# First FFN norm: eight ones-matmuls a quarter become one, with the squares added up on VectorE and GpSimd

## What is computed

```python
def rmsnorm(x, w):
    xf = x.astype(jnp.float32)
    y = xf * lax.rsqrt(jnp.mean(xf * xf, axis=-1, keepdims=True) + EPS)
    return (y * w.astype(jnp.float32)).astype(x.dtype)

def swiglu(h, w_gate, w_up, w_down):
    return (jax.nn.silu(h @ w_gate) * (h @ w_up)) @ w_down

x = x + (0.5 * swiglu(rmsnorm(x, p['norm_ffn1']), ...)).astype(x.dtype)
```

## Time and profile before

| | us |
|---|---|
| median of three runs (2019.36 to 2021.33) | 2020.1 |
| the profiled execution, own time | 2022.36 |
| its span in the profile | 2020.5 |
| TensorE matmuls busy in the span | 1983.1 (98%) |
| VectorE / ScalarE / GpSimd busy | 1184.3 / 780.5 / 229.9 |

### The profile page before, as it was taken

One profiled execution on the slowest core, in us unless ns is written; L12 is line 12 of the kernel. 1 busy time (PEld: TensorE's weight loads), 2 busy tenths in 40 slices (PEclk: granted clock), 3 DMA queues, 4 the chain that ended last, 5 costly groups with the idle time before them and its releaser, 6 DMA issues.

```text
span 2020.5 us, 36315 instructions
## 1 busy us (share of the span) xinstructions
PE 1983.1 (98%) x15393; PEld 1928.7 (95%) x15393; DVE 1184.3 (59%) x1640; ACT 780.5 (39%) x1268; POOL 229.9 (11%) x285
## 2 busy tenths in 40 slices
PE   7999999999999999999999999999999999999999
PEld 7899999999999989868899989999999999999999
DVE  5955655556776752565354283377555565577674
ACT  6433333334433342564333393243333333343331
POOL 0000000000000340250011162100000000000000
PEclk9999999999999999999999999999999999999999
DMA  4222232224976515211011133312322223388664
GB/s 153 81 87 102 87 115 96 87 102 175 372 278 235 211 43 192 83 50 43 25 42 43 58 90 130 133 45 100 116 87 84 100 100 116 117 316 324 251 218 161
DMA packets 67042, 265.05 MB, mean 131 GB/s; under 512 B 7564, under 2 KB 20284, under 8 KB 57536
## 3 DMA queue, kind: packets, MB, share of 16 engines
q1 hardware_dynamic: 51648, 198.89, 27.2%
q0 software_dynamic: 15232, 63.83, 8.2%
HBM read 203.52 MB, written 59.18 MB: 130 GB/s over the span
## 4 chain that ended last, share of the span: by engine, by line
PE 92%; DVE 4%; ACT 3%; issue 1%; DMA 1%; POOL 0%; SPq 0%; DVEq 0%; ACTq 0%
PE ps L169 85%; PE ps L1485 1%; PE ps L1529 1%; PE ps L1511 1%; PE ps L247 1%; DVE sb_x L509 0%; DVE sb_xl L563 0%; PE ps L2123 0%; PE ps L2111 0%; PE ps L2089 0%; DVE sb_xl L499 0%; DMA sb_x<-x 0%; PE ps L2105 0%; PE ps L2116 0%; DVE sb_x L548 0%
## 5 line engine op out<-in xcount | busy, mean ns | idle before, releaser
L169 PE MATMUL ps<-sb_xh,sb_up_hi 128*128 128x272 f32 x2400 | 691.9, 288 | 6.4 <-DVE sb_x L2448 2.0
L169 PE MATMUL ps<-sb_xl,sb_up_hi 128*128 128x272 f32 x2400 | 692.2, 288 | 0.0
L169 PE MATMUL ps<-sb_xh,sb_up_lo 128*128 128x272 f32 x2400 | 690.2, 288 | 0.0
L169 PEld LDWEIGHTS ps<-sb_xh,sb_up_hi 128*128 128x128 f32 x2400 | 453.0, 189 | 7.8 <-DVE sb_up_lo L454 2.3
L169 PEld LDWEIGHTS ps<-sb_xh,sb_up_lo 128*128 128x128 f32 x2400 | 452.5, 189 | 0.0
L169 PEld LDWEIGHTS ps<-sb_xl,sb_up_hi 128*128 128x128 f32 x2400 | 452.2, 188 | 0.1
L169 PE MATMUL ps<-sb_h_hi,sb_down_hi 128*128 128x272 f32 x1188 | 342.6, 288 | 0.4 <-DVE sb_down_lo L1049 0.4
L169 PE MATMUL ps<-sb_h_hi,sb_down_lo 128*128 128x272 f32 x1188 | 342.7, 288 | 0.0
L169 PE MATMUL ps<-sb_h_lo,sb_down_hi 128*128 128x272 f32 x1188 | 341.8, 288 | 0.0
L169 PE MATMUL ps<-sb_nh,sb_whi 128*128 128x362 f32 (+1 forms) x696 | 231.0, 332 | 2.4 <-DVE sb_nl L376 1.5
L169 PE MATMUL ps<-sb_nl,sb_whi 128*128 128x362 f32 (+1 forms) x696 | 228.3, 328 | 0.0
(11 more groups left out here) (334 smaller groups left out, 2692.3 us busy)
## 6 DMA issues: line engine op xcount, KB each, us to landing
sb_down_raw<-wb SPq DMA_DIRECT2D x92, 704.0 KB, 5.4
sb_up_raw<-wa SPq DMA_DIRECT2D x44, 1024.0 KB, 4.9
sb_h_raw<-h_kept SPq DMA_DIRECT2D x60, 544.0 KB, 6.1
sb_wraw<-wm SPq DMA_DIRECT2D x17, 1024.0 KB, 4.8
h_kept<-sb_hs_b POOLq DMA_DIRECT2D x20, 816.0 KB, 5.3
h_kept<-sb_hbuf POOLq DMA_DIRECT2D x42, 272.0 KB, 2.3
h_kept<-sb_hs_a POOLq DMA_DIRECT2D x20, 544.0 KB, 3.2
sb_h_first_raw<-h_kept SPq DMA_DIRECT2D x10, 544.0 KB, 4.8
```

The lines of the kernel that those rows point to most:

```text
L169: mm = K.nc.tensor.matmul(out, a, b, start=first and n == 0, stop=last and n == 2, skip_group_check=loose)
```

## The change

VectorE now adds up the squares of quarter 0 and of quarter 3 (three instructions each). GpSimd makes the squares of quarter 1 itself, as a product of `x` with `x` in one instruction of 128 x 2176 elements, once that quarter has landed, into a buffer of its own (`sq_second`); then it adds up the squares of quarter 2, and then those of quarter 1, with a wait on its own semaphore between the steps. ScalarE no longer squares quarter 1. TensorE sums each quarter with one matmul: those of quarters 2, 3 and 0 all stand behind k = 3 of c = 1, that of quarter 1 behind k = 7. On ScalarE the root of quarter 0 moves ahead of the cast of item 0, and `root(1)` behind that cast.

```diff
 FIRST_SUMS = (2, 3, 0, 1)
-SQUARED = (0, 2, 3, 1)
+SQUARED = (0, 2, 3)
...
-    if c == 0:
-        e.wait_ge(N.f.added, N.was.added + 1)
-        mm = K.nc.tensor.matmul(K.ps[:, bank, :Q], K.ones, first_squares(K, c)[:, 0], start=True, stop=True)
+    if c in (0, 3):
+        e.wait_ge(N.f.added, N.was.added + (0, 3).index(c) + 1)
     else:
-        for k in range(KT):
-            if k % 4 == 0:
-                e.wait_ge(N.f.sq, N.was.sq + 2 * SQUARED.index(c) + k // 4 + 1)
-            mm = K.nc.tensor.matmul(K.ps[:, bank, :Q], K.ones, first_squares(K, c)[:, k], start=k == 0,
-                                    stop=k == KT - 1)
-    mm.then_inc(N.f.sum_mm, 1)
+        e.wait_ge(N.f.pool_added, 4 if c == 2 else 7)
+    K.nc.tensor.matmul(K.ps[:, bank, :Q], K.ones, first_squares(K, c)[:, 0], start=True, stop=True)\
+        .then_inc(N.f.sum_mm, 1)
...
+def first_pool(K, e, N):
+
+    step = Chain(e, N.f.pool_added)
+
+    def add(t):
+        step(K.nc.gpsimd.tensor_tensor(t[:, 0:4], t[:, 0:4], t[:, 4:8], ALU.add))
+        step(K.nc.gpsimd.tensor_tensor(t[:, 0:2], t[:, 0:2], t[:, 2:4], ALU.add))
+        step(K.nc.gpsimd.tensor_tensor(t[:, 0], t[:, 0], t[:, 1], ALU.add))
+
+    x = K.x[:, :, QUARTERS[1][0]:QUARTERS[1][1]]
+    e.wait_ge(K.x_in[1], 16)
+    step(K.nc.gpsimd.tensor_tensor(K.sq_second[:], x, x, ALU.mult))
+    e.wait_ge(N.f.sq, N.was.sq + 2 * SQUARED.index(2) + 2)
+    add(first_squares(K, 2))
+    add(first_squares(K, 1))
...
     root(2)
-    squares(1, (0,))
     root(3)
-    squares(1, (4,))
+    root(0)
 
     def after(i):
         if i == 0:
-            root(0)
-        if i == 1:
             root(1)
...
-            if c == 1 and k in (0, 2, 5, 6):
-                first_sum_pe(K, e, N, {0: 2, 2: 3, 5: 0, 6: 1}[k])
+            for quarter in {3: (2, 3, 0), 7: (1,)}.get(k, ()) if c == 1 else ():
+                first_sum_pe(K, e, N, quarter)
...
             unscaled_lo(K, e, F1, V_N1, 0, range(4, KT))
+            first_sum_dve(K, e, F1, M, 0)
             unscaled_lo(K, e, F1, V_N1, 1, range(4))
-            first_sum_dve(K, e, F1, M)
+            first_sum_dve(K, e, F1, M, 3)
             unscaled_lo(K, e, F1, V_N1, 1, range(4, KT))
...
+            first_pool(K, e, F1)
             up_pool(K, e, F1, o["h_kept"], x_in)
```

More of the change, by code:

```diff
@@ L228, with first_sum_dve @@
 FIRST_SUMS = (2, 3, 0, 1)
-SQUARED = (0, 2, 3, 1)
+SQUARED = (0, 2, 3)
 def first_squares(K, c):
-    return K.sq_third if c == 3 else K.sq_first[:, 0:KT] if c == 0 else K.sq_first[:, KT:2 * KT]
+    return (K.sq_first[:, 0:KT], K.sq_second, K.sq_first[:, KT:2 * KT], K.sq_third)[c]
 def first_sum_pe(K, e, N, c):
     bank = 4 + FIRST_SUMS.index(c)
-    if c == 0:
-        e.wait_ge(N.f.added, N.was.added + 1)
-        mm = K.nc.tensor.matmul(K.ps[:, bank, :Q], K.ones, first_squares(K, c)[:, 0], start=True, stop=True)
-    else:
-        for k in range(KT):
-            if k % 4 == 0:
-                e.wait_ge(N.f.sq, N.was.sq + 2 * SQUARED.index(c) + k // 4 + 1)
-            mm = K.nc.tensor.matmul(K.ps[:, bank, :Q], K.ones, first_squares(K, c)[:, k], start=k == 0,
-                                    stop=k == KT - 1)
-    mm.then_inc(N.f.sum_mm, 1)
-def first_sum_dve(K, e, N, M):
-    t = first_squares(K, 0)
-    e.wait_ge(N.f.sq, N.was.sq + 2)
+    if c in (0, 3):
+        e.wait_ge(N.f.added, N.was.added + (0, 3).index(c) + 1)
+    else:
+        e.wait_ge(N.f.pool_added, 4 if c == 2 else 7)
+    K.nc.tensor.matmul(K.ps[:, bank, :Q], K.ones, first_squares(K, c)[:, 0], start=True, stop=True)\
+        .then_inc(N.f.sum_mm, 1)
+def first_sum_dve(K, e, N, M, c):
+    t = first_squares(K, c)
+    e.wait_ge(N.f.sq, N.was.sq + 2 * SQUARED.index(c) + 2)
     M.dve(K.nc.vector.tensor_tensor(t[:, 0:4], t[:, 0:4], t[:, 4:8], ALU.add))
@@ L295, in squares @@
         e.wait_ge(K.x_in[c], 16)
-        if c == 1:
-            e.wait_ge(N.f.sum_mm, N.was.sum_mm + 1)
         for k in ks:
@@ L2487, in __init__ @@
         self.added = sem("ffn_added")
+        self.pool_added = sem("ffn_pool_added")
         self.sum_mm = sem("ffn_sum_mm")
@@ L2523, in __init__ @@
     def __init__(self, norms, done):
-        self.sq = (0, 2 * 4, 2 * 4 + NPC * KT)[norms]
-        self.added = (0, 1, 1 + NPC * (KT - 2))[norms]
+        self.sq = (0, 2 * 3, 2 * 3 + NPC * KT)[norms]
+        self.added = (0, 2, 2 + NPC * (KT - 2))[norms]
         self.sum_mm = (0, 4, 4 + NPC)[norms]
@@ L2737, in hybrid_layer @@
         K.sq_first = at("sq_first", XL + 2 * 4 * HALF, [16, Q])
+        K.sq_second = at("sq_second", XL + X_B11 * 4 * HALF, [KT, Q])
         K.sq_third = at("sq_third", WA + 8192, [KT, Q])
```

## The result

The changed kernel takes 2023.87 us (median of 21 runs, 2021.34 to 2026.93) against 2020.89 us of the kernel before in the same session: ratio 1.0013, 95% interval 1.0007 to 1.0019. By that ratio it is 2.6 us slower, 1.4 to 3.8 (the two medians lie 3.0 us apart). The time lies inside the stated range only because the second rival had set its lower end at 2021.5; the forecast's own bounds, 2024.2 to 2027.8, begin just above it.

What follows compares the result with a forecast made beforehand. Item 2's subtraction, fed by VectorE and GpSimd in turns, was taken to bound the kernel: 4.2 us later quarter 1 sum plus 1.35 us root order gave +5.5, 2025.6 us on a 2020.1 median; stated range 2021.5 to 2028.5.

Steps and rivals of the forecast that it cites:

- the second rival: VectorE/GpSimd sharing: only tensor_tensor takes turns, low parts run beside GpSimd; about 2022 us, chance 0.10.
- the forecast's own bounds: Whole kernel: +4.1 to +7.7 us from unknown handovers and clock stretches, 2024.2 to 2027.8 us around 2025.6.
- what bounds it: Start of the kernel: item 2's subtraction at 38.08 us sets the unbroken matmuls from 97.00; any shift reaches the end.
- The rule that VectorE and GpSimd take turns: Between 12 and 37 us: VectorE instructions with two SBUF inputs alternate with GpSimd's 14 us of SBUF-reading work.
- no turns: First rival, VectorE/GpSimd sharing: GpSimd's work lies beside VectorE's; -6.2 us, 2013.9 us, chance 0.08.
- the order of the roots: ScalarE: item 1's cast now waits for quarter 1's sum, putting one subtraction and one normalisation behind it; +1.35 us.
- the sum of quarter 1: TensorE: quarter 1's ones-matmul ends at 40.7 instead of 36.54 us, 4.2 us later.
- The product: GpSimd: squaring quarter 1, 2176 elements at 2.15 ns each, takes 4.84 us from about 13.6.
- The handovers: VectorE/GpSimd turns: 13 handovers saving 0.13 us each; turns end between 30.4 and 32.1, taken as 31.2.
- The clock: TensorE before quarter 1's first matmuls: one stretch at clock 0.50 after some 6 us idle; 1.3 us lost.
- The low parts of quarter 0: VectorE: four low parts spread from 13.6 to about 24 us, one nearly 5 us long.
- The price that only a page gives: GpSimd: first call of freshly loaded code may pay about 6 us; if after quarter 1 lands, time near 2027.

Runs made afterwards that it cites:

- all ten traces of the table: Traces of the kernel before, the changed kernel and its variants (root order, busy TensorE, sums or squares moved); timed ratios 0.9973 to 1.0013.
- the clock out of the way: 52 extra matmuls keep TensorE busy, in the changed kernel (ratio 1.0013) and in the changed kernel with the old root order (1.0000).
- the first trace of the changed kernel: Changed kernel, nothing else altered, VectorE's add first at 18.8; item 2's subtraction at 40.65 us, timed ratio 1.0013.
- in the second: Second trace of the unaltered changed kernel, GpSimd's add first (18.42 before 18.54); item 2's subtraction at 40.90 us, not timed.
- the first probe: Kernel before plus five extra GpSimd instructions at the start (memset, a*a, a*b, a+a, a+b on 544 columns); a*a took 1.09 us, a*b 1.33.

## Why the prediction was right in sign and too large

**Right: what bounds it.** In all ten traces of the table the long piece starts 58.9 us behind the subtraction of item 2. That the gain or loss reaches the end in full is shown by the ratios alone, within their intervals. The rule that VectorE and GpSimd take turns holds for scalar_tensor_tensor and tensor_tensor alike: the first low part beside the product took 4.06 us for 0.50 and ended 0.30 us after it.

```profile
13.70 4.06 DVE L288 SCALAR_TENSOR_TENSOR sb_x_unscaled_lo<-sb_x,sb_vec,sb_x_unscaled_hi 128x272 fp32r<-128x272 f32 x1
```

So "no turns" falls. "Only tensor_tensor takes turns" gave about 2022, nearer to the measured time than the forecast, but that low part refutes it: its number was right for a wrong reason.

**Right: the order of the roots.** 1.35 predicted, 1.33 measured with the clock out of the way; in the first trace of the changed kernel the delay of the wait itself is 1.22 (ScalarE's root of quarter 1 starts at 37.79, before at 36.57), and the rest of the 2.57 is the order.

**Mis-sized: the sum of quarter 1.** It was to end at 40.7 and ended at 37.75, 1.2 us later than before instead of 4.2. Three terms of that sum are off, by 1.2, 1.3 and 0.5 us, which is the missing 3.0.

- *The product.* 4.84 us by the rate of operations on two tensors; it held VectorE up for 13.78 to 17.45, 3.67 us. The earlier trace rows have no operation of a tensor with itself. 1.2 us too much. The prediction had named this as a sign of being wrong: GpSimd's rate on 2176 elements is not that of 1024.
- *The handovers.* The stretch of turns was taken as 31.2 + 1.73 - 13.6 = 19.3 us up to the fourth low part of quarter 1; it took 16.8. With 1.2 for the product the other 1.3 are handovers. GpSimd's adds behind a VectorE instruction took 2.38, 1.19 and 0.61 where alone they take 2.50, 1.33 and, by the slope of the earlier trace rows, 0.76: close to the 0.13 us of the earlier trace rows, each time. But VectorE's instructions gain too: a low part ends 0.30 us after GpSimd, where one takes 0.50 by itself, an add of 544 elements 0.58 instead of 0.72. I had taken the middle between full saving and none; a bit more than full saving was right, and it was in the earlier trace rows, where the low part ended 0.40 after GpSimd instead of 0.59.
- *The clock.* 1.3 us of slow clock were charged, of which 0.5 reached the sum (35.9 against the 35.4 of quarter 3's sum). The slow stretch is there (6.7 us at 0.50 in the first trace), but in that trace it lay beside VectorE's work and cost nothing; in the second it cost 0.4.

Behind that, quarter 3's sum came 2.44 us after the turns, as priced, and TensorE's 24 matmuls took 3.00 us for the 2.9 of the sum. Smaller differences cancel: one of the three ones-matmuls ran while TensorE waited for quarter 3's sum.

**Wrong in the details.** The low parts of quarter 0 were to spread until 24; they were done at 18.99, since the product ended early and GpSimd's next instruction had to wait for squares until 18.64. TensorE's longest idle time was 4.5 or 6.8 us long and ended at 25.6 or 27.9, not at 31.7.

**The price that only a page gives.** The Trainium skill (GPSIMD Engine Reference, 2.1 Instruction dispatch) states a load of about 6 us at the first call of freshly loaded code. Neither the product (issued at 13.20, it had ended 4.25 us later) nor the first probe (1.09 us, like the third) shows it. Whether such a load went on unseen before them the traces don't tell. For the sum the measurement decides: nothing is added.

**Left open.** Why GpSimd mostly goes first at 18.8 (five of six traces with these turns, each time 0.12 or 0.13 us ahead) and VectorE once, with the same lead of GpSimd, no trace tells.

## What to carry to other kernels

An idle engine is not free help. Ask first whether its instruction reads SBUF beside VectorE instructions with two SBUF operands: then its time is added to VectorE's, at GpSimd's slower rate. A sum that VectorE does in 2.44 us cost VectorE 3.8 us of stretched instructions when GpSimd did it (7.5 us for the two sums of the changed kernel). Work is better put on an engine that waits and shares no turn, here TensorE (3.8 us for eight ones-matmuls, beside VectorE). And look at what stands behind a moved wait on its engine: two lines of order cost as much as the rest of the change.

## What the runs showed of the hardware that I had not expected

A GpSimd operation of a tensor with itself takes 1.09 us on 128 x 544, with two tensors 1.33. GpSimd's memsets cost VectorE nothing (5.86 us beside it). Which of the two engines gets the turn can differ between executions of one program, and with it the time at which others start: 18.79 and 18.91 gave VectorE first, 18.42 and 18.54 GpSimd first. Far behind the change TensorE's clock makes differences between two traces that are half as large as the change's own: the same 60 matmuls took 9.29 us at a mean clock of 0.66 and 7.77 at 1.00 (clock of the stretch 1311 to 1316).
